# Two-part rounding of every weight chunk, and five side loads spread over one stage

## The reference

```
def swiglu_ffn(h, w_in, w_out):
    g, u = jnp.split(h @ w_in, 2, axis=-1)
    return (jax.nn.silu(g) * u) @ w_out
...
    for layer in range(DEPTH):
        mod = (jax.nn.silu(c) @ ada_w[layer] + ada_b[layer]).reshape(B, 3, 3, D)
        h = modulate_pre(x, g[0, 0], mod[:, 0, 0], mod[:, 0, 1])
        y = swiglu_ffn(h, ffn_w_in[layer, 0], ffn_w_out[layer, 0])
        x = gated_post_add(x, y, g[0, 1], mod[:, 0, 2], 0.5)
        ...
...
        proj = h @ w_in[l]
        x = x + gt1 * (merged @ w_out[l])
        hidden = jnp.square(jax.nn.relu(h2 @ w_ff1[l]))
        x = x + gt2 * (hidden @ w_ff2[l])
```

## Time and profile before

| | |
|---|---|
| time, median of 3 runs | 2091.6 us (2090.18 to 2093.61) |
| the profiled execution's own time | 2096.16 us |
| its span, first to last instruction | 2094.3 us |
| PE busy | 2048.9 us, 98% |
| DVE busy | 1539.5 us, 74% |
| ACT busy | 1039.2 us, 50% |
| TensorE clock granted, mean | 0.992 |

### The profile page before, as it was taken

How to read it: one execution, slowest core, us unless ns; L and a number is a source line. 1 busy time by engine, 2 the same in 40 slices (tenths; PEclk the granted TensorE clock), 3 DMA queues, 4 the chain that set the end, 5 groups by cost and what they waited for, 6 DMA issues and landing times.

```text
span 2094.3 us, 39039 instructions
## 1 busy us (share of the span) xinstructions
PE 2048.9 (98%) x16760; PEld 2004.9 (96%) x16760; DVE 1539.5 (74%) x1918; ACT 1039.2 (50%) x1209; POOL 233.9 (11%) x355
## 2 busy tenths in 40 slices
PE   8999999999999999999999999999999999999998
PEld 8999999999999997999999999999998999999998
DVE  7788889788778889688875466677888455757554
ACT  5544545335643467543454443355446454346443
POOL 0111101111411110111110100011111000001000
PEclk9999999999999999999999999999999999999999
DMA  9898656996799940489846554558996455545663
GB/s 352 313 343 306 221 201 232 342 356 211 236 328 371 361 152 25 131 317 328 311 157 199 183 189 162 162 191 307 368 340 202 161 191 185 176 162 172 214 220 120
DMA packets 265549, 497.37 MB, mean 237 GB/s; under 512 B 17185, under 2 KB 146593, under 8 KB 265122
## 3 DMA queue, kind: packets, MB, share of 16 engines
q1 hardware_dynamic: 230354, 366.42, 51.6%
q0 software_dynamic: 35024, 128.47, 16.3%
HBM read 491.16 MB, written 1.05 MB: 235 GB/s over the span
## 4 chain that ended last, share of the span: by engine, by line
PE 79%; DVE 8%; DMA 4%; ACT 4%; SPq 2%; issue 1%; POOL 1%; DVEq 0%; ACTq 0%; POOLq 0%
PE PB L584 8%; PE PB L586 8%; PE PA L584 8%; PE PB L585 8%; PE PA L586 7%; PE PA L585 7%; PE PY L584 7%; PE PY L586 7%; PE PY L585 7%; DVE wlo L1701 2%; ACT whi L1218 2%; DMA raw<-ffn_w_in 2%; SPq L451 1%; PE PA L624 1%; PE PA L617 1%
## 5 line engine op out<-in xcount | busy, mean ns | idle before, releaser
L1701 DVE TENSOR_TENSOR wlo<-raw,whi 128x2048 fp32r<-128x2048 f32 x327 | 750.1, 2303 | 335.4 <-ACT whi L1218 334.4
L1218 ACT ACTIVATE whi<-raw 128x2048 fp32r<-128x2048 f32 x321 | 612.1, 1912 | 497.3 <-DMA raw<-ffn_w_in 211.6
L584 PE MATMUL PY<-opB_hi,whi 128*128 128x256 f32 x1344 | 378.4, 282 | 9.8 <-DVE wlo L1701 6.6
L586 PE MATMUL PY<-opB_hi,wlo 128*128 128x256 f32 x1344 | 375.4, 279 | 0.0
L585 PE MATMUL PY<-opB_lo,whi 128*128 128x256 f32 x1344 | 375.3, 279 | 0.0
L584 PE MATMUL PA<-opA_hi,whi 128*128 128x256 f32 x1120 | 317.8, 284 | 7.6 <-DVE wlo L1701 5.4
L586 PE MATMUL PA<-opA_hi,wlo 128*128 128x256 f32 x1120 | 316.8, 283 | 0.0
L585 PE MATMUL PA<-opA_lo,whi 128*128 128x256 f32 x1120 | 315.8, 282 | 0.0
L584 PE MATMUL PB<-opA_hi,whi 128*128 128x256 f32 x1024 | 289.8, 283 | 2.4 <-DVE wlo L1701 2.4
L586 PE MATMUL PB<-opA_hi,wlo 128*128 128x256 f32 x1024 | 289.1, 282 | 0.0
L585 PE MATMUL PB<-opA_lo,whi 128*128 128x256 f32 x1024 | 288.1, 281 | 0.0
(11 more groups left out here) (374 smaller groups left out, 3937.9 us busy)
## 6 DMA issues: line engine op xcount, KB each, us to landing
raw<-ffn_w_in SPq DMA_DIRECT2D x176, 512.0 KB, 6.6
scr<-adat POOLq DMA_DIRECT2D x160, 512.0 KB, 6.5
raw<-w_in SPq DMA_DIRECT2D x144, 512.0 KB, 4.5
raw<-w_ff SPq DMA_DIRECT2D x128, 512.0 KB, 4.7
raw<-ffn_w_out SPq DMA_DIRECT2D x88, 512.0 KB, 5.9
adaw<-adat POOLq DMA_DIRECT2D x80, 512.0 KB, 6.6
raw<-w_branch SPq DMA_DIRECT2D x48, 512.0 KB, 4.5
raw<-a_w_in SPq DMA_DIRECT2D x24, 512.0 KB, 4.7
```

The source lines that it names most:

```text
L584: nc.tensor.matmul(o_, w1, rhs(xh), start=start, stop=False, skip_group_check=True)
L586: return nc.tensor.matmul(o_, w2_, rhs(xh), start=False, stop=stop, skip_group_check=True)
L1218: AC(whi[slot][:, 0:w], raw[slot][:, 0:w], ACT.Copy).then_inc(hi_ready, 1)
L1701: TT(wlo[slot][:, 0:w], raw[slot][:, 0:w], whi[slot][:, 0:w].bitcast(F32), ALU.subtract).then_inc(lo_ready, 1)
```

## The change

It makes two edits. First, ACT rounds a chunk by two instructions of 1024 columns instead of one of 2048, each raising `hi_ready` by one, and DVE subtracts in two instructions, the first waiting for the first half alone; `lo_ready` still rises once a chunk, after the second half. The counts of `hi_ready` double everywhere (the first eight chunks raise it by two). Where ACT rounded a chunk in four pieces between other work (`prep_part`), the pieces stay and the counter rises after the second and the fourth. Second, the five side loads of ffn01 no longer stand together ahead of in5: `t_nsa` goes ahead of in4, `pos2` ahead of in6, `w2k` ahead of in7 and in8, `w2v` ahead of in9.

```
-                    if name == "ffn01" and (kind, j) == ("in", 5):
+                    if name == "ffn01" and (kind, j) == ("in", 4):
                         sp.wait_ge(multiplied, CH["conv_out"] + 4)
                         sp.dma_start(tnsa, I["t_nsa"]).then_inc(nsa_in, 16)
+                    if name == "ffn01" and (kind, j) == ("in", 6):
                         sp.dma_start(pos2, I["cmp_pos2"]).then_inc(cmp_in, 16)
-                        for u in range(2):
-                            sp.dma_start(w2k[:, :, 64 * u:64 * u + 64], w2[0]).then_inc(cmp_in, 16)
+                    if name == "ffn01" and (kind, j) in (("in", 7), ("in", 8)):
+                        u = j - 7
+                        sp.dma_start(w2k[:, :, 64 * u:64 * u + 64], w2[0]).then_inc(cmp_in, 16)
+                    if name == "ffn01" and (kind, j) == ("in", 9):
                         sp.dma_start(w2v, w2[1]).then_inc(cmp_in, 16)
...
             def prep(c, w):
...
-                AC(whi[slot][:, 0:w], raw[slot][:, 0:w], ACT.Copy).then_inc(hi_ready, 1)
+                for i in range(2):
+                    sl_ = slice(i * w // 2, (i + 1) * w // 2)
+                    AC(whi[slot][:, sl_], raw[slot][:, sl_], ACT.Copy).then_inc(hi_ready, 1)
...
+                if i % 2:
+                    ins.then_inc(hi_ready, 1)
                 if i == 3:
-                    ins.then_inc(hi_ready, 1)
...
             def split(slot, w=CHUNK):
-                TT(wlo[slot][:, 0:w], raw[slot][:, 0:w], whi[slot][:, 0:w].bitcast(F32), ALU.subtract).then_inc(lo_ready, 1)
+                for i in range(2):
+                    dve.wait_ge(hi_ready, 2 * nxt[0] + 1 + i)
+                    sl_ = slice(i * w // 2, (i + 1) * w // 2)
+                    ins = TT(wlo[slot][:, sl_], raw[slot][:, sl_], whi[slot][:, sl_].bitcast(F32), ALU.subtract)
+                ins.then_inc(lo_ready, 1)
...
-                    dve.wait_ge(hi_ready, nxt[0] + 1)
```

More of the change, by code:

```diff
@@ L480, in ffn @@
                     p_ = c0 + FFN_AT[kind, j]
-                    if name == "ffn01" and (kind, j) == ("in", 5):
+                    w2 = I["cmp_w2"].rearrange("k (m p) d -> k p m d", p=P)
+                    if name == "ffn01" and (kind, j) == ("in", 4):
                         sp.wait_ge(multiplied, CH["conv_out"] + 4)
                         sp.dma_start(tnsa, I["t_nsa"]).then_inc(nsa_in, 16)
+                    if name == "ffn01" and (kind, j) == ("in", 6):
                         sp.dma_start(pos2, I["cmp_pos2"]).then_inc(cmp_in, 16)
-                        w2 = I["cmp_w2"].rearrange("k (m p) d -> k p m d", p=P)
-                        for u in range(2):
-                            sp.dma_start(w2k[:, :, 64 * u:64 * u + 64], w2[0]).then_inc(cmp_in, 16)
+                    if name == "ffn01" and (kind, j) in (("in", 7), ("in", 8)):
+                        u = j - 7
+                        sp.dma_start(w2k[:, :, 64 * u:64 * u + 64], w2[0]).then_inc(cmp_in, 16)
+                    if name == "ffn01" and (kind, j) == ("in", 9):
                         sp.dma_start(w2v, w2[1]).then_inc(cmp_in, 16)
@@ L1441, in ffn_first @@
                         else:
-                            ins.then_inc(hi_ready, 1)
+                            ins.then_inc(hi_ready, 2)
                     if k:
@@ L2030, in ffn_first @@
                         else:
-                            dve.wait_ge(hi_ready, k + 1)
+                            dve.wait_ge(hi_ready, 2 * k + 2)
                         sl_ = slice(512 * j, 512 * end)
```

## The result

The changed kernel takes **2078.2 us** (median of 5 runs, 2077.83 to 2080.84); the kernel before, on the same chip, 2091.6 (5 runs, 2087.78 to 2093.61). The ratio is 0.994, interval 0.9927 to 0.9953: 10 to 15 us less. The profiled execution has a span of 2076.4 us against 2094.3.

The account below looks back on a forecast made before the run. PE, busy 98% of the span, bounds the kernel, so only its waits and low clock can yield. Terms of 10.3 us less 0.7 of losses give 9.6; from the median 2091.6 that makes 2082.0, range 2077 to 2090.

Parts of the forecast that it names:

- (a): At ffn01+13: moving the side loads ends PE's 2.4 us wait and the low clock behind it; gain 3.7 us.
- rivals one and three: One (0.20): in ffn01 the wait only moves, 2085 us. Three (0.06): each separate small load delays its chunk, 2106 us.
- (b): In ffn00: all of PE's 1.3 us wait goes, since three splits in a row each waited for ACT.
- (f): In ff0: PE's wait for one chunk late from DMA goes whole, 0.5 us.
- (c): Second step of ffn01 and of ffn11: a split that waited for ACT ends earlier; together 1.2 us.
- (d): In cmp: two waits, 1.1 us, follow splits that wait for ACT; gain 1.0 us.
- (e): Chunk 5 of ff0 and ff1: waits of 2.4 us each shrink to 1.6; gain 1.5 us together.
- the 0.76 us of the earlier trace: Wherever DVE waits for ACT, a chunk in halves is ready 0.76 us earlier, if DVE was idle that long.
- (g): Chunk 8 of mix0 and mix1: the rotation starts earlier, so PE waits 0.55 us less each, together 1.1.
- Losses: Splits on PE's chains that do not wait cost 0.07 us each, ACT's 0.11; ten links allowed, 0.7 us.
- Rival two: Everywhere: the halves do little, as splits that did not wait pay 0.07 us each; about 2090 us, chance 0.12.
- the 2.45: On DVE: by the skill's formula two half splits would take 2.45 us, 0.16 more than the whole.

## Why the prediction was right, and by which errors

The direction and the time (2082.0 forecast, 2078.2 measured, 13.4 less instead of 9.6) held, but with luck, through errors that offset each other: 3.7 us were laid to the loads and 5.9 (9.6 - 3.7) to the halves, where the loads alone gave 0.4 (-1.9 to 2.7) and the halves alone 11 to 12.

- **(a), mis-sized.** The step "the chunk lands some 5 us earlier and 2.4 is covered twice" is right in its mechanism: 7.1 instead of 11.7 to 14.6 us to landing. Its size was read from one execution in which the chunk came later than it does otherwise. The side loads made no new wait in any place, so rivals one and three did not come about.
- **(b) and (f)** do not stand in the second profile. (b) came back in the run with halves only at the boundaries (1.3 us) and without overlap (1.7), so it comes and goes; (f) stood in the first profile alone.
- **(c), (d), (e)** were right, 3.9 us found for 3.7, and stand in both profiles of before: here the 0.76 us of the earlier trace rows carries over directly.
- **(g)** was right, in mechanism and size: 0.6 us at each place for the 0.55 forecast, once the time of POOL's copy is taken out. The forecast left open that the copy "can meet other transfers", and that is what hid it: 1.70 and 1.79 in the first profile of the changed kernel, but 1.43 and 1.33 with the halves alone, where the forecast said 1.3 and 2.4. The 3.0 in mix1 was a slow copy; it stood again (2.98) with the loads alone, and was 1.90 in the second profile of before.
- **The boundaries, left out.** The sum went by waits that end on `wlo`. The four on `accy` hang on a split too, some links further back. 3 x 0.87 = 2.6 us of them repeat; the fourth, at conv_in, was 1.1 us in the first profile alone (0.3 or less elsewhere).
- **The clock, counted once of seven.** I priced the low clock behind (a), and gave the others no place in the sum. In the first profile of before, 0.50 was granted seven times before the last chunk, in the changed kernel's twice. Over 59 runs of the kernel before, timed beside the experiments, the 31 with a mean clock of 0.994 or less took 2089.8 to 2096.9 us, the 28 with more 2084.3 to 2093.2; all 11 of the changed kernel have 0.997 or more. The median of these clocks is 0.994 for before and 0.997 for the changed kernel, and between before's median times at 0.993 (2093.9) and at 0.996 (2089.0) lie 4.9 us. That fewer and shorter waits keep the clock up is shown at the three boundaries (the counts stand in the last section); that it makes up a part of the whole gain is argued, since no run set the clock alone. It can't be most of it: before's 19 runs at 0.996 or 0.997 have a median of 2089.0 us, still some 10 us above the changed kernel's eight at 0.997 (2078.7).
- **From the profile to the median.** The sum was one of the first profile's waits, and the distance of 4.6 us between that execution and the median was taken to stay. It did not: the changed kernel's profiled execution lies at its median (2078.19 and 2078.2). Profile against profile the gain was 17.9 us, almost twice the 9.6; against medians, 13.4.
- **Losses, too low.** 0.07 us a link was right only where DVE runs alone. At the start of ff0 and ff1 the pair took 3.44 us instead of 2.83, for POOL's adds between the halves.
- **Rival two** had a point, but the wrong sign of the sum: without overlap the cut costs some 10 us over all splits, and the overlap pays more. What its 163 splits cost alone no run shows.
- The pair took 2.36 us as in the earlier trace rows. The Trainium skill, VectorE: DVE Perf Modes, section "The TRN2 errata — SBUF-src ops pay a fixed extra latency per instruction", has a formula that agrees with one instruction (1224 ns, 1232 measured here). But two in a row overlap by some 0.1 us, so the 2.45 did not come.

## What to carry to other kernels

A wait behind a DMA queue changes with the execution: take two profiles before you put 40% of a gain on one row, and trust the waits that stand in both to the hundredth. Where a wait hangs on a transfer, subtract the transfer's own time before you compare; what was left at chunk 8 of mix0 and mix1 stood to 0.02 us from profile to profile. List PE's waits by what they hang on, several links back, and not by the releaser's name alone; here about a third of the waits that went or shrank stood under another name. Cut a producer in parts where its consumer waits for it, and leave it whole where the consumer is late for its own reasons or shares its time with GpSimd.

## What the runs showed of the hardware

The clock falls behind long waits more than behind short ones, but not behind each wait of a size. At the boundaries ahead of ffn01, ffn11 and mix0, over the thirteen profiles, 0.50 (the lower level, 1.2 GHz) was granted behind ten of the fifteen waits of 1.06 to 1.16 us and behind none of the 21 of 0.19 to 0.41. In ff0, 2.40 us of idle PE left it at 1.00 in the run with the loads alone, and it fell in another (halves at the boundaries only); 1.07 us at a boundary brought it down twice out of three times in the second profile of before. Windows of that profile, from the wait ahead of ffn01 on:

```profile
306.40:309.80 3.40, 2.50 (x21) 0.99 0.78 246
309.80:313.20 3.40, 3.40 (x18) 0.50 0.20 67
313.20:316.60 3.40, 3.40 (x31) 1.00 0.00 0
```

There it costs only some 0.6 us (the step at that boundary is 1.51 with it, against 0.88 at mix0 without), since PE has little to do then. Dearer is a stretch in the mixer nsa that the first profiles of both kernels did not have: in the second profile of the changed kernel the clock fell after 1.49 us of waiting, and that cost 3.2 us. The same 1.49 us stand in all thirteen profiles, and the clock fell behind them in eight. The windows are of that run, and of the changed kernel's first profile at the same place:

```profile
767.20:774.00 6.80, 6.80 (x49) 0.50 0.01 2
```
```profile
764.90:771.70 6.80, 6.79 (x79) 1.00 0.04 15
```

So two executions of one program differ by 3 us at a single place, with the same wait ahead of it.
